# The modulation product as fp32 multiply-adds on VectorE inside the two feed-forward blocks, in place of a TensorE stage

## The reference

```python
x = rmsnorm(x, g_final)                       # end of the first block
x = x + sincos_2d(...)                        # start of the second
shift1, scale1, gate1, shift2, scale2, gate2 = split(silu(c) @ w_ada + b_ada, 6)
cshift, cscale = split(silu(c_ctx) @ w_ada + b_ada, 6)[0:2]
h  = rmsnorm(x,   g_pre_mix) * (1 + scale1) + shift1
hc = rmsnorm(ctx, g_pre_mix) * (1 + cscale) + cshift
y  = token_mix(h, hc)                         # begins with h @ w_in_2, hc @ w_in_2
x  = x + gate1 * rmsnorm(y, g_post_mix)
h2 = rmsnorm(x, g_pre_ffn) * (1 + scale2) + shift2
x  = x + gate2 * rmsnorm(hier_moe(h2), g_post_ffn)
```

## Time and profile before

| | us |
|---|---|
| median of 3 runs | 1369.15 (1367.84 to 1369.71) |
| span of the profiled execution | 1367.6 |
| TensorE busy | 1209.1 (88%) |
| VectorE busy | 958.6 (70%) |
| ScalarE busy | 717.0 (52%) |
| GpSimd busy | 233.0 (17%) |
| transfers | 251.40 MB, mean 184 GB/s |
| mean granted TensorE clock | 0.932 of full |

### The profile page before, as it was taken

The page is one execution under the profiler, slowest core; times in us unless marked ns, Lnnn a source line. Parts: engine busy times, 40 slices in busy tenths (PEclk is TensorE's granted clock), DMA queues, the critical chain, the costliest instruction groups (busy, mean ns, idle before and its releaser), DMA issues.

```text
span 1367.6 us, 19000 instructions
## 1 busy us (share of the span) xinstructions
PE 1209.1 (88%) x6784; PEld 1008.1 (74%) x6784; DVE 958.6 (70%) x1435; ACT 717.0 (52%) x995; POOL 233.0 (17%) x183
## 2 busy tenths in 40 slices
PE   4876979999885867999999799998669999999996
PEld 4656779999784756999994249567558888888885
DVE  5799565555469975655548884446689888898887
ACT  4332544444343234544426564452457888887885
POOL 4625000000137230000004350025510000000000
PEclk9987899999978969999999889999679999999999
DMA  9214014555903040455579740110517877778774
GB/s 383 104 62 185 0 62 185 184 188 184 367 24 123 15 171 1 154 187 185 187 310 391 301 171 1 62 62 1 245 46 279 327 279 299 307 281 324 277 283 155
DMA packets 21380, 251.40 MB, mean 184 GB/s; under 512 B 2886, under 2 KB 3014, under 8 KB 4682
## 3 DMA queue, kind: packets, MB, share of 16 engines
q1 hardware_dynamic: 21324, 250.68, 47.4%
HBM read 249.62 MB, written 1.05 MB: 183 GB/s over the span
## 4 chain that ended last, share of the span: by engine, by line
PE 72%; DVE 15%; issue 8%; ACT 2%; DMA 1%; POOL 1%; DVEq 0%; SPq 0%; POOLq 0%; ACTq 0%
PE bank L642 21%; PE bank L644 20%; PE bank L643 20%; PE bank L633 3%; PE bank L1130 2%; PE bank L1147 2%; DVE scratch L1695 2%; DMA m<-in_w_in 1%; DVE w_l L1655 1%; DVE h_l L1661 1%; DVE w_l L1922 1%; DVE w_l L2102 1%; PE bank L993 1%; DVE scratch L1749 1%; DVE scratch L1744 1%
## 5 line engine op out<-in xcount | busy, mean ns | idle before, releaser
L2102 DVE TENSOR_TENSOR w_l<-m,w_h 128x1024 fp32r<-128x1024 f32 x196 | 238.9, 1250 | 20.6 <-ACT w_h L1537 19.9
L644 PE MATMUL bank<-h_h,fw_l 128*128 128x256 f32 x800 | 224.2, 280 | 0.0
L642 PE MATMUL bank<-h_h,fw_h 128*128 128x256 f32 x704 | 199.4, 283 | 8.5 <-DVE h_l L1866 8.5
L1537 ACT ACTIVATE w_h<-m 128x1024 fp32r<-128x1024 f32 x200 | 198.0, 1051 | 15.8 <-DMA m<-in_experts 15.7
L643 PE MATMUL bank<-h_l,fw_h 128*128 128x256 f32 x704 | 197.6, 281 | 0.0
L1854 DVE TENSOR_TENSOR fw_l<-blocks_w,fw_h 128x1024 fp32r<-128x1024 f32 x132 | 153.5, 1218 | 0.0
L644 PEld LDWEIGHTS bank<-h_h,fw_l 128*128 128x128 f32 x800 | 152.0, 190 | 0.0
L642 PEld LDWEIGHTS bank<-h_h,fw_h 128*128 128x128 f32 x704 | 133.2, 189 | 10.7 <-issue 9.0
L1878 DVE TENSOR_TENSOR acts<-acts,bank 128x256 f32<-128x256 f32 x44 | 18.5, 420 | 173.6 <-ACT acts L1362 173.6
L643 PEld LDWEIGHTS bank<-h_l,fw_h 128*128 128x128 f32 x704 | 133.8, 190 | 1.8
L1362 ACT ACTIVATE acts<-bank 128x256 f32<-128x256 f32 x44 | 16.9, 384 | 222.8 <-PE bank L644 222.8
(11 more groups left out here) (382 smaller groups left out, 2907.0 us busy)
## 6 DMA issues: line engine op xcount, KB each, us to landing
m<-in_experts SPq DMA_DIRECT2D x50, 2048.0 KB, 7.3
blocks_w<-in_ffn SPq DMA_DIRECT2D x22, 2048.0 KB, 7.4
m<-in_w_in SPq DMA_DIRECT2D x11, 2048.0 KB, 14.0
blocks_w<-in_ffn SPq DMA_DIRECT2D x22, 1024.0 KB, 4.9
m<-in_w_ada SPq DMA_DIRECT2D x8, 2048.0 KB, 12.0
m<-in_w_out SPq DMA_DIRECT2D x6, 2048.0 KB, 7.1
blocks_w<-in_w_ada SPq DMA_DIRECT2D x4, 2048.0 KB, 9.0
blocks_w<-in_w_in SPq DMA_DIRECT2D x2, 2048.0 KB, 18.7
```

The costliest lines, as they stand in the source:

```text
L642: pe.matmul(out_, xh, wh, start=first and i == 0, stop=False, skip_group_check=True)
L644: ins = pe.matmul(out_, xl, wh, start=False, stop=last and i == n - 1, skip_group_check=True)
L1537: act.activation(w_h[:, c % 3, at], m[:, c % 4, at], ACT.Copy).then_inc(hi_ready, 1)
L2102: dve.tensor_tensor(w_l[:, c % 4, at], m[:, c % 4, at], f32(w_h[:, c % 3, at]), ALU.subtract).then_inc(lo_ready, 1)
```

## The change

1. The row tiles and the split form of the product go. `w_ada` is laid out as 12 chunks of 512 columns; `acc`, a tile of 128 partitions by 4096 columns for each layer, starts as the bias in its first partition and zeros elsewhere (a 2 MB load each). In the FFN of layer 0 VectorE accumulates the parts shift1 and scale1 for both condition vectors, in that of layer 1 the remaining four parts for the latent one. For each partition p it adds w[p, n] * c[p]: 64 multiply-adds of 512 columns per layer (`ada_rows`), eight in each of blocks 0 to 7, placed between the rests of that block, in plain fp32. SP loads 1 MB per block in layer 0 and 2 MB in layer 1 (`ada_part`), each behind the loads of an FFN block.
2. TensorE sums over partitions afterwards: behind each FFN, 32 (layer 0) and 16 (layer 1) plain fp32 matmuls with a 128 x 128 stationary part of `acc` and one column of ones, and for the gates four matmuls of ones against 512 columns (`gate0` to `gate3`, behind the `tl` transposes). VectorE turns the first into the modulation columns (`modulation`), and multiplies the gates by their gains.
3. Moved into the second FFN: the context rows' load, squares and norm, and the rounding and the rests of the first input projection weights (`rounded_columns(0)`, `rest_of_columns(0)`, all on ScalarE and VectorE). silu(c) moves to the start of layer 0 on ScalarE, behind a load of `prm2`.
4. Final norm, gain, position and second norm of x follow directly behind the second FFN.
5. The loops over layers, and inside the FFN those of SP, ScalarE and VectorE, are written out; TensorE's loop over the FFN's blocks stays.
6. In layer 1 the load of `guv` waits for layer 0's modulation matmuls, those of `vqi` and `qk` for its multiply-adds.

```diff
@@ SP, per layer
+                def ada_part(b):
+                    if b >= 2:
+                        sp.wait_ge(ada_step, ADA_STEPS * l + 8 * (b - 1))
+                    half = slice(2048 * (b % 2), 2048 * (b % 2 + 1))
+                    if l == 0:
+                        sp.dma_start(m[:, 0, half], a["w_ada"][b // 2, :, half]).then_inc(ada_in[b % 2], 16)
+                    else:
+                        for j in range(2):
+                            sp.dma_start(m[:, b % 2, 2048 * j:2048 * (j + 1)],
+                                         a["w_ada"][4 + b // 2 * 2 + j, :, half]).then_inc(ada_in[b % 2], 16)
...
+                res.ready(sp, "wo3")
+                sp.dma_start(acc[l], a["b_ada"][l]).then_inc(acc_in, 16)
+                ada_part(0)
+                ada_part(1)
+                if l == DEPTH - 1:
+                    for t in range(NT):
+                        sp.dma_start(ctx_x[:, t, :], a["ctx"][t * P:(t + 1) * P, :]).then_inc(ctx_in, 16)
+                for b in range(2, NFB):
+                    next_block(b, b % 2, B1 * l + b // 2 + b % 2)
+                    if b < ADA_BLOCKS:
+                        ada_part(b)
+            sp.wait_ge(ada_step, ADA_STEPS * DEPTH)
+            for s in range(2):
+                sp.dma_start(m[:, s, :], a["w_in_2"][s]).then_inc(m_in[s], 16)
+            sp.wait_ge(block_used[1], B1 * DEPTH + 1)
+            sp.dma_start(gfin, a["g_final"].partition_broadcast(P)).then_inc(pos_in, 16)
             sp.dma_start(pos.rearrange("p t d -> p (t d)"), a["pos"]).then_inc(pos_in, 16)
+            sp.dma_start(gb.rearrange("p q d -> p (q d)"), a["g_post"].partition_broadcast(P)).then_inc(gains_in, 16)
@@ TensorE, behind each FFN
+                pe.wait_ge(ada_step, ADA_STEPS * (l + 1))
+                res.room(pe, "mod")
+                for n in range(2):
+                    for k in range(KD):
+                        for row in range(2 - l):
+                            at = ((4 * row + 2 * n if l == 0 else 2 + 2 * n) + k // 4) * 512 + k % 4 * P
+                            o = (n * KD + k) * 2 + row
+                            ins = pe.matmul(to("mod")[:, o:o + 1], acc[l][:, at:at + P], const[:, K_ONES:K_ONES + 1],
+                                            start=True, stop=True)
+                res.done(ins, "mod")
...
-            with pe.Fori(0, 2) as i:
-                for s in range(ADA):
...
-                        ins = split_chain(bank[s][0:2, :], ...)
...
             transposes2("tc", XN + 1, ctx_x)
             transposes2("tl", XN + 3, xn2)
+            for n in range(4):
+                sec.room(pe, f"gate{n}")
+                at = (n + n // 2 * 4) * 512
+                sec.done(pe.matmul(to(f"gate{n}")[:, :], const[:, K_ONES:K_ONES + P], acc[1][:, at:at + 512],
+                                   start=True, stop=True), f"gate{n}")
@@ ScalarE, FFN and behind it
+                for b in range(NFB - 1):
+                    ffn_silu(0, b)
+                    rounded((b + 1) % 2, (b + 1) // 2, range(0, 4))
+                    ffn_silu(1, b)
+                    rounded((b + 1) % 2, (b + 1) // 2, range(4, 6))
+                    if l == DEPTH - 1 and b == 2:
+                        act.wait_ge(ctx_in, 32)
...
+                ffn_silu(0, NFB - 1)
+                if l == DEPTH - 1:
+                    rounded_columns(0, xm_h)
+                ffn_silu(1, NFB - 1)
...
+            for t in range(NT):
+                layer_results(DEPTH - 1).arrived(act, f"y{2 * t + 1}")
+                act.activation(junk[:, t, :], x[:, t, :], ACT.Square, accum_out=ss[:, t:t + 1]).then_inc(ss_ready, 1)
+            for t in range(NT):
+                act.wait_ge(x_ready, t + 1)
+                act.wait_ge(ss_ready, 4 * DEPTH + 2 + t + 1)
+                act.activation(junk[:, t, :], x[:, t, :], ACT.Square, accum_out=ss[:, t:t + 1]).then_inc(ss_ready, 1)
@@ VectorE, FFN and behind it
+                def ada_rows(b, k):
+                    if k == 0:
+                        dve.wait_ge(ada_in[b % 2], 16 * (b // 2 + 1) if l == 0 else 64 + 32 * (b // 2 + 1))
+                    for j in range(2):
...
+                        n = ADA_STEPS * l + 8 * b + 2 * k + j
+                        if n > 1:
+                            dve.wait_ge(ada_step, n - 1)
+                        part, c = acc[l][:, chunk * 512:(chunk + 1) * 512], 4 * (b % 2) + k
+                        dve.scalar_tensor_tensor(part, w[:, k * 512:(k + 1) * 512], cs[:, c, row:row + 1], part, ALU.mult, ALU.add)\
+                            .then_inc(ada_step, 1)
+                dve.wait_ge(silu_c, 1)
+                dve.wait_ge(acc_in, 16 * (l + 1))
+                for b in range(NFB - 1):
+                    ffn_hidden(0, b)
+                    for n in range(4):
+                        rest_of_block((b + 1) % 2, b + 1, (n,))
+                        if b < ADA_BLOCKS and n >= 2:
+                            ada_rows(b, n - 2)
+                    ffn_hidden(1, b)
+                    for n in range(4, 6):
+                        rest_of_block((b + 1) % 2, b + 1, (n,))
+                        if b < ADA_BLOCKS:
+                            ada_rows(b, n - 2)
...
+                ffn_hidden(0, NFB - 1)
+                if l == DEPTH - 1:
+                    rest_of_columns(0, xm_h, (0, 1))
+                ffn_hidden(1, NFB - 1)
+                if l == DEPTH - 1:
+                    rest_of_columns(0, xm_h, (2, 3))
                 add_to_x("y")
...
+            modulation(1)
+            dve.wait_ge(pos_in, 32)
+            for t in range(NT):
+                dve.wait_ge(rstd_ready, 4 * DEPTH + 2 + t + 1)
+                S.then(dve.scalar_tensor_tensor(x[:, t, :], x[:, t, :], rstd[:, t:t + 1], gfin, ALU.mult, ALU.mult))
+                dve.tensor_tensor(x[:, t, :], x[:, t, :], pos[:, t, :], ALU.add).then_inc(x_ready, 1)
+            dve.wait_ge(x_ready, 2)
             normed(4, x, xn2, 0)
...
             rest_of_rows(0, h_l, hC, hc_h)
+            dve.wait_ge(gains_in, 16)
+            for n in range(4):
+                sec.ready(dve, f"gate{n}")
+                part = gb[:, n // 2, n % 2 * 512:(n % 2 + 1) * 512]
+                sec.moved(dve.tensor_tensor(part, part, bank[4 + n][:, :], ALU.mult), f"gate{n}")
             rest_of_rows(1, hl_l, hT, h1_h)
```

More of the change, by code:

```diff
@@ L36 @@
 NMOD = 6
-ADA = 6
+ADA_BLOCKS, ADA_STEPS = 8, 64
 NE, EPG, NG = 16, 4, 4
@@ L107, in layer_banks @@
         b.add(n, f"y{n}")
+    b.add(6, "mod")
     return b
@@ L112, in second_banks @@
     b = Banks()
-    for s in range(ADA):
-        b.add(s, f"ada{s}", times=NMOD * D // 512 // ADA)
-    b.add(6, "modT")
-    for s in range(4):
-        b.add(s, f"gate{s}")
     for n in range(4):
@@ L121, in second_banks @@
         b.add(n, f"tl{n}")
+    for s in range(4):
+        b.add(4 + s, f"gate{s}")
     for j in range(4):
@@ L376, in build @@
         fT = again.take(4, T)
-        modc = again.take(4, KD, 2)
         w_rt = again.take(KD, NG + NE)
@@ L413, in build @@
         y2 = rounded_place("y2", "yT", 0, 2, D)
-        ctx_x = Region(scratch, N_SCRATCH, ctx_at).take(NT, D)
+        ctx_x, ctx_junk = (Region(m[:, 3, :], 4096, n * NT * D).take(NT, D) for n in range(2))
+        junk = Region(scratch, N_SCRATCH, ctx_at).take(NT, D)
         tmp = Region(scratch, N_SCRATCH, ctx_at).take(4, 512)
@@ L647, in _ @@
             pe.wait_ge(const_in, 16)
-            with pe.Fori(0, DEPTH) as l:
+            for l in range(DEPTH):
                 res = layer_results(l)
@@ L912, in _ @@
-            for s in range(ADA):
-                sec.arrived(pe, f"ada{s}", 1)
-            sec.room(pe, "modT")
-            for n, row in enumerate((0, 1, 3, 4)):
-                for k in range(KD):
-                    ins = pe.transpose(to("modT")[:, 2 * (KD * n + k):2 * (KD * n + k) + 2],
-                                       modrow[:, row * D + k * P:row * D + (k + 1) * P], ident[0:2, 0:2])
-            sec.done(ins, "modT")
-            def gate(q):
-                pe.wait_ge(gate_rows, q + 1)
-                for n in (2 * q, 2 * q + 1):
-                    o = (2 + 3 * q) * D + (n % 2) * 512
-                    sec.room(pe, f"gate{n}")
-                    sec.done(pe.matmul(bank[n][:, :], ident[0:2, 0:1].to_broadcast([2, P]), modrow[:, o:o + 512],
-                                       start=True, stop=True), f"gate{n}")
@@ L1227, in _, with rounded_columns @@
         def _(act):
+            def rounded_columns(s, high):
+                act.wait_ge(m_in[s], (M01, M01, M23)[s] + 16)
+                if s == 0:
+                    act.wait_ge(block_used[1], B1 * DEPTH + 1)
+                for j in range(4):
+                    at = slice(j * 1024, (j + 1) * 1024)
+                    act.activation(high[:, at], m[:, s, at], ACT.Copy).then_inc(w2_hi, 1)
             act.wait_ge(x_in, 16 * NT)
-            with act.Fori(0, DEPTH) as l:
+            for l in range(DEPTH):
```

(22 more changed lines are left out.)

242 lines of the change are left out of this document (51 added, 191 removed).

## The result

The changed kernel takes 1292.87 us (median of 4 runs, 1292.11 to 1293.9) against 1369.43 of the kernel before beside it (1367.84 to 1370.98): ratio 0.944, 95% interval 0.9426 to 0.9453. A second series gave 1291.6 against 1371.33, ratio 0.9417 (0.9403 to 0.943). The forecast was 1292.6, range 1285 to 1307. The span of the profiled execution went from 1367.6 to 1292.1, against 1291.1 in the sum. The total was right to about a us, and that is partly luck: several of its terms were off by 1 to 3 us each, in opposite directions, as the part on the prediction shows.

A forecast was written before the change was run, and what follows sets the result against it. TensorE was taken to bound both FFNs, with 96 us of product and x's chain between FFN and projection. 1367.6 - 77.0 + 0.5 = 1291.1 us of span, plus 1.55 to the median: 1292.6, range 1285 to 1307.

The forecast's parts named there:

- the sum: Whole profiled execution: 1367.6 - 77.0 + 0.5 = 1291.1 us of span; 1292.6 as median of the runs.
- Part 1: Both FFNs: the product's multiply-adds on VectorE, 0.75 us each, 15.2 of a block's 16.87 us, cost nothing.
- The rival on longer FFNs: Both FFNs: late gate loads and VectorE near its limit together give 1298 to 1317, middle 1305; chance 0.17.
- Part 2: Both FFNs: 1 or 2 MB more of transfers per block cost nothing, between 0 and 10 us in all.
- Part 3: Matmuls behind the FFNs: 32 behind layer 0 take 7.9 us, delaying the whole by +0.5, from -1 to +7.
- The gap: TensorE's idle time before layer 1's first transpose, taken as 6.1 us, to hold most of the 32 matmuls.
- Part 5: Moved context and weight work, silu(c) at the start, written-out loops: all nothing, within 1 us each way.
- longer chain: Rival: modulation matmuls behind layer 0 run at low clock, +7, giving 1299; chance 0.08.
- Part 4: From F, the second FFN's last matmul: `xm` starts at F+19.5 and ends at 769.6, 77.0 us earlier.
- the tail: The rest behind `xm`, to the end of the kernel: keeps its length.
- VectorE as the bound: Rival: multiply-adds of 16 FFN blocks make it slower, eating all 77 us from 1.56 us each; chance 0.02.
- GpSimd at work: FFNs: the only condition said to make multiply-adds slow enough; at 2 us a piece the time is 1426.

The follow-up runs named there:

- the change's second profile: The changed kernel run once more without any edit, as measure for the three kernels beside it: 1291.6 us, ratio 0.9417.
- the narrow run: Against the changed kernel, all 128 multiply-adds cover one column instead of 512, with waits and transfers kept: 1292.28 us, ratio 0.9421.
- the new order: Changed kernel with context transposes, modulation matmuls, then latent transposes behind the second FFN; context modulated between x's squares: 1294.67 us, ratio 0.945.

## Why the prediction was right

- **Part 1 (multiply-adds free):** right. 0.747 us a piece against 0.75, period 16.88, and the narrow run shows that nothing of it reaches the end. Its working had one flaw that only more load could show: it added durations of records where VectorE's pace is set by the distance between starts. The cover is 2.6 us a block (16.87 - 14.3), not 1.7. (The rival on longer FFNs books 92% of VectorE's time and 75% of the transfer rate; by the prediction's own numbers these are 15.2 / 16.87 = 90% and 311 / 406 = 77%.)
- **Part 2 (transfers free):** right. ScalarE waits 3.8 us for loads, and TensorE not at all. The margin is not large: 30% more per block, two thirds of it from memory to memory, costs 10 us.
- **Part 3 (matmuls behind layer 0):** the mis-sized term. Forecast +0.5 in a range of -1 to +7; measured +3.1 at the second FFN's last down load (698.58 to 701.71). Three of its steps failed. The price: 0.31 us each and not 0.25, since the clock fell during them; I had argued that TensorE "has just run at full clock". The gap: 2.5 us were left of the 6.1. And "its readers stand behind VectorE's two norms, 5.62 us long": the first of these took 0.75 us, so that TensorE and not VectorE became late. Part 5's "no branch wait of mine is on the chain" covered up the same point: something at the turn of the layer did change. The rival "longer chain" had named the low clock, for all 32 and at +7.
- **Part 4 (the chain behind F):** right in kind, 2 us too long. F+17.4 against F+19.5. Second gain and position ended at F+8.8 (9.5), the second norm at F+11.8 (12.4), the latent transposes at F+14 (14.4), the context's low parts at F+16.7 (17.6), and the gates let `xm` start at F+17.4 (18 to 21.4): each step ended 0.3 to 1 us earlier than its forecast. That low parts and gate matmuls would end together was right; the new order took the low parts away and showed that the gates alone hold the time nearly as long. The end of `xm` was forecast at 769.6 and came at 769.5, and that is luck: F came 3.1 us late, the chain was 2.1 us short, and `xm` itself took 22.5 us and not 23.6, since the low clock that had been allowed for at its start did not come (the granted clock is 1.00 from 744 to 751).
- **Part 5 and the tail:** `xm` to the end was 520.8 us before and 522.6 after, 519.1 in the change's second profile (769.80 to 1288.9); beside the clock falls I see no change there. The profile in which the sum fits to 1 us has these falls; without them the span is 1288.9.
- **Rivals:** VectorE as the bound exists, but from a higher point: with 0.66 us a piece 8 multiply-adds leave 2.6 us, and 16, twice the work, cost 50 of the 77 us gained. The condition "GpSimd at work" also holds, at 4.9 us a block where three additions run.

## What to carry to other kernels

Work moved under an engine that bounds a stage costs nothing as long as the receiving engine's starts, not the durations of its records, fit the stage's period; add twice the work and look whether the period moves to learn how much cover is left. The steps that stay at the seam are where such a change is won or lost: ask for each gap on which it relies whether the change itself closes it, here by an engine that comes to its turn earlier. After a chain is shortened, an engine that waits in it can take the chain's later, independent work, as the gate matmuls did.

## What the runs showed of the hardware

- TensorE's granted clock fell from 1.00 to 0.50 in the midst of 64 fully busy records of one moving column (2.00 us busy in each 2 us stretch), in each of eight profiles, and stayed at 1.00 with 128 columns in the same place (both kernels with all 32 matmuls there). The narrower form was the slower one: 10.05 us against 7.31.
- A plain fp32 matmul of one column costs as much as one of 128 at the full clock, 0.227 against 0.228 us.
- Two profiles of one kernel differed by 3.0 us through two clock falls of some microseconds each; a difference of that size between single profiles is no finding.
- VectorE's records overlap: 0.747 us long, 0.664 apart (512 columns, three operands), and 1.22 long, 1.14 apart (1024 columns, two). The pace of a full engine is the second number.
